# Product u in split parts, with VectorE's low parts at fixed places inside the convolution

## The chip, the cores and the metric

The kernel runs on one core of one Trainium2 chip. The metric is the time of one execution on the device in microseconds (us). The kernel before took 1014.25 us (median of three runs, 1013.29 to 1018.42).

## The reference, cut to what matters

One layer of a streaming encoder: 512 prompt tokens and 32 sample tokens (544 together), model width 1024, all in 32-bit floats.

```
h = modulate(rms_norm(x), shift, scale)
z = h @ w_in + b_in                    # 1024 -> 6 * 1024: a (2 parts), u, v, gates (2 parts)
a = glu(z[a]); a = silu(layer_norm(depthwise_causal_conv(a, width 31)))
u, v = gelu(z[u]), gelu(z[v]); v = layer_norm(v)
y_b = (u * (w_s mixes v over 128-frame chunks)) @ w_b
y_a = a @ w_a
merged = sigmoid(z[gate A]) * y_a + sigmoid(z[gate B]) * y_b
x = x + g1 * (merged @ w_o)
x = x + g2 * hierarchical MoE(modulate(rms_norm(x)))   # 32 experts
y = modulate(rms_norm(x))
```

## The kernel before, in words

The five engines' programs are written out by hand, each in its own order, and meet at semaphores. The features lie on partitions: a 1024x544 matrix is eight tiles of 128x544. TensorE makes the input projection in this order: eight units for a (each unit is two products, the value and the gate half of one tile), the product for v, four units for u (two tiles each), then sixteen gates, two to a unit. Between the gates stand the transposes of the convolution's history (`histories`), the channel statistics (`over_features`) and the mixing matrices (`mix`). After that come the two branch projections with the modulation products between them, the output projection, the routing and the experts.

Two forms of product are in use. `product` (L509 on) takes the 32-bit operands as they are: eight steps over the inner dimension, two halves of 272 columns each, and each such matmul is two records of L515 in the trace. `product_split` (L575 on, matmul at L580) works on parts: a high part (the operand rounded to the format `fp32r`) and a low part (the operand less its high part, in the same format). It runs three matmuls in place of each one: high weights with high input, high weights with low input, low weights with high input. The kernel before uses it for the gates alone.

Weights of the input projection go through two buffers (`W`, `WP`, the same memory), 1 MB a unit. SP loads unit n once `w_used` says that TensorE is done with unit n - 2 (`unit_load`). The high parts of a unit's weights (`wH2`) lie in the second half of its buffer, the low parts (`wL2`) replace the weights in place. For the gates ScalarE makes the high parts (`high_gate`, copy at L978, counted in `gw_high`) and GpSimd the low parts (`low_gate`, L1605, counted in `gw_split`). The parts of the input h are `gH` (ScalarE, L955, all eight tiles after the last unit of a, counted in `g_high`) and `gL` (VectorE, L1243, all eight tiles after the convolution's sums, counted in `g_split`). `gate(0)` waits for `g_split`.

VectorE runs the depthwise convolution in a hardware loop (`Fori`, L1211) of four turns, two channel tiles a turn: four multiplies for the GLU (L1217), two `tensor_scalar` for tap 0 (L1225), and 60 `scalar_tensor_tensor` for taps 1 to 30 (L1228), each over 574 columns; every address in the loop comes from registers. After it come the sums over tiles (`add_tiles`, L1234, counted in `conv_sum`), `gL`, the statistics of v (L1249, L1250, counted in `v_var`), then, once ScalarE has taken the square roots (L1004, L1005), the reciprocal (L1255) and the normalised v (L1259, L1264, L1265), of which GpSimd does a share (L1613, L1615). Then the channel means are subtracted (L1269) and the mixed v is added and multiplied into u (L1278, L1281, L1284). L643 is the first matmul of `mix` and waits for `v_norm`.

ScalarE drains each product: L948 and L949 for a, L973 for v, L985 for u, L997 for the gates. After `gate(0)` it stores a history (L961 and a DMA at L963), then waits for `v_var` and takes the square roots, then goes on with `gate(1)` and the second history. TensorE's `over_features` (L650) waits for that second history copy.

Of the kernel before, what the change touches and what calls it, by code (L numbers as in the profile page):

```python
# [29 lines left out]
ds = bass.ds  # L30
# [41 lines left out]
def build(nc, a, y_out, hist_p_out, hist_s_out, v_out):  # L72
    with ExitStack() as ctx:
# [153 lines left out]
        w_full = [sem("w_full0"), sem("w_full1")]  # L227
        x2_in = sem("x2_in")
        bias_split, conv_sum = sem("bias_split"), sem("conv_sum")
        glu_ready, gate_ps, gate_drained, y_ps = sem("glu_ready"), sem("gate_ps"), sem("gate_drained"), sem("y_ps")  # L230
# [277 lines left out]
        def _(pe):  # L508
# [110 lines left out]

            pe.wait_ge(v_gelu, 10)  # L620
            for n in range(4):
                b = n % 2
                full(pe, U_U + n)
                pe.wait_ge(act_drained, Q_U + n - 1)
                for m in range(2):
                    last = product(4 * b + 2 * m, WP[b][:, m], hT)
                last.then_inc(w_used, 1)
# [256 lines left out]
        def _(act):  # L884
# [59 lines left out]
            for n in range(KT):  # L944
                b = 4 * (n % 2)
                act.wait_ge(w_used, U_A + n + 1)
                for bank, c0, w, at in ((b, 0, H, HIST), (b + 1, 0, NPROMPT - H, HIST + H), (b + 1, NPROMPT - H, NSAMPLE, 2 * HIST + NPROMPT)):
                    act.activation(aF[:, n, at:at + w], PS[:, bank, c0:c0 + w], ACT.Identity, bias=VT[:, COL_BIN + n:COL_BIN + n + 1]).then_inc(glu_ready, 1)  # L948
                act.activation(two(cv[:, n, 0:T]), PS[:, b + 2:b + 4, 0:H], ACT.Sigmoid,  # L949
                               bias=VT[:, COL_BIN + KT + n:COL_BIN + KT + n + 1]).then_inc(act_drained, 1)  # L950
            act.wait_ge(h_even, KT)
            act.wait_ge(h_odd, KT)
            act.wait_ge(bias_split, 3)
            for j in range(KT):
                act.activation(gH[:, j, :], hT[:, j, :], ACT.Copy).then_inc(g_high, 1)  # L955

# [8 lines left out]
            for g, (what, bank) in enumerate(zip(V_ORDER, V_BANK)):  # L965
                if g in (4, 8):
                    act.wait_ge(w_used, U_V + 1 + g // 8)
                else:
                    act.wait_ge(v_ps, g + 1 if g < 4 else g)
                for hf in (0, 1) if g == 2 else (what[1],):  # L970
                    src = PS[NSAMPLE * hf:NSAMPLE * (hf + 1), bank + hf, :] if g == 2 else PS[:, bank, :]
                    t = 4 if g == 2 else what[0]
                    act.activation(v[0:WIDTH[t], t, hf * 512:(hf + 1) * 512], src, ACT.Gelu_apprx_tanh).then_inc(v_gelu, 1)  # L973

            def high_gate(q):
                full(act, U_G + q)
                for m in range(2):
                    act.activation(wH2[q % 2][:, m], WP[q % 2][:, m], ACT.Copy).then_inc(gw_high, 1)  # L978

            for n in range(4):  # L980
                b = n % 2
                act.wait_ge(w_used, U_U + n + 1)
                for m in range(2):
                    j = 2 * n + m
                    last = act.activation(two(uT[:, j, :]), PS[:, 4 * b + 2 * m:4 * b + 2 * m + 2, 0:H], ACT.Gelu_apprx_tanh,  # L985
                                          bias=VT[:, COL_BIN + 2 * KT + j:COL_BIN + 2 * KT + j + 1])
                last.then_inc(act_drained, 1)
                if n == 2:
                    high_gate(0)

# [8 lines left out]

            high_gate(1)  # L1000
            gate(0)
# [119 lines left out]
        def _(dve):  # L1121
# [88 lines left out]

            with dve.Fori(0, KT // 2) as half:  # L1211
                i = half * 2
                dve.wait_ge(act_drained, i + (Q_A + 2))
                dve.wait_ge(glu_ready, i * 3 + 6)
                for b in range(2):
                    for at, w, first in ((HIST, NPROMPT, 0), (2 * HIST + NPROMPT, NSAMPLE, NPROMPT)):
                        dve.tensor_tensor(tile_of(aF, i + b, at, w), tile_of(aF, i + b, at, w), tile_of(cv, i + b, first, w),  # L1217
                                          ALU.mult).then_inc(aF_written, 1)
                dve.wait_ge(aF_written, i * 2 + 8)
                for k in range(TAPS):  # L1220
                    for b in range(2):
                        total, src = tile_of(cv, i + b, 0, CONV), tile_of(aF, i + b, k, CONV)
                        tap = VT[:, ds(i + (k * KT + b), 1)]
                        if k == 0:
                            dve.tensor_scalar(total, src, tap, VT[:, ds(i + (COL_CB + b), 1)], ALU.mult, ALU.add).then_inc(conv_step, 1)  # L1225
                        else:
                            dve.wait_ge(conv_step, i * TAPS + (2 * (k - 1) + b + 1))
                            dve.scalar_tensor_tensor(out=total, in0=src, scalar=tap, in1=total, op0=ALU.mult, op1=ALU.add).then_inc(conv_step, 1)  # L1228


# [9 lines left out]
            add_tiles(cv)  # L1240
            dve.wait_ge(g_high, KT)
            for j in range(KT):
                dve.tensor_tensor(gL[:, j, :], hT[:, j, :], gH[:, j, :], ALU.subtract).then_inc(g_split, 1)  # L1243
            dve.wait_ge(bc_in, 64)
# [325 lines left out]
        def _(pool):  # L1570
# [31 lines left out]
            def low_gate(q):  # L1602
                for m in range(2):
                    pool.wait_ge(gw_high, 2 * q + m + 1)
                    pool.tensor_tensor(wL2[q % 2][:, m], WP[q % 2][:, m], wH2[q % 2][:, m], ALU.subtract).then_inc(gw_split, 1)  # L1605
# [118 lines left out]
```

## Time and profile before

| What | Value |
|---|---|
| Median of three runs | 1014.25 us |
| The profiled execution's own time | 1014.02 us |
| Its span | 1012.2 us |
| Mean granted TensorE clock | 0.944 of full speed |
| TensorE matmul busy | 886.8 us, 88% |
| TensorE weight load busy | 619.2 us, 61% |
| VectorE busy | 464.1 us, 46% |
| ScalarE busy | 169.2 us, 17% |
| GpSimd busy | 150.1 us, 15% |
| HBM read, written | 206.31 MB, 15.37 MB |

The span runs from the first to the last instruction of the profiled execution; the execution's own time is 1.8 us more. Busy time is the union of an engine's instructions. In the rows further down, a timeline row gives start, duration, engine, line, operation, written and read tiles, shape and count; consecutive instructions of one form are merged, and the bracket gives the idle time of the engine ahead of the row and what ended it. Two instructions of one engine can overlap by a little, since the next starts while the last one's results are still being written.

### The profile page before, as it was taken

To read this page: it belongs to the slowest core of one execution; us is meant where nothing else is said; L and a number is where in the kernel's file an instruction comes from. 1 tells how busy PE (TensorE), PEld (TensorE's weight loads), DVE (VectorE), ACT (ScalarE), POOL (GpSimd) and SP (SyncE) were. 2 spreads that over 40 slices of the span, in tenths; PEclk is the share of its full clock that TensorE was granted. 3 is DMA by queue.
4 is the path that set the end of the run, shared out by engine and by line. 5 is a ranking of instruction groups with operands and counts; after the bars stand their busy time and mean duration, and the time that the engine had idled before them with its cause. 6 is when DMAs were issued, how large, how long until landed. Compare 5 with 4: busy or idle time off the path is not lost. (4 is left out here: it accounts for less than half of the span.)

```text
span 1012.2 us, 11883 instructions
## 1 busy us (share of the span) xinstructions
PE 886.8 (88%) x4633; PEld 619.2 (61%) x4636; DVE 464.1 (46%) x694; ACT 169.2 (17%) x262; POOL 150.1 (15%) x180
## 2 busy tenths in 40 slices
PE   2899999999997979899999999817998898877846
PEld 1688885348887979776666544515666565544512
DVE  2329999999929361201112143571332233223127
ACT  3210113100142114500000011201121111101003
POOL 2000000000047083001111000002222222121110
PEclk9899999999998989999999999757999999989877
DMA  9912333003322133646758391434999999999943
GB/s 326 299 54 73 84 92 116 25 17 84 84 76 64 43 125 84 218 158 260 286 203 297 113 344 41 157 130 168 417 419 417 416 404 410 365 376 414 368 158 130
DMA packets 96116, 210.41 MB, mean 208 GB/s; under 512 B 10412, under 2 KB 52756, under 8 KB 87358
## 3 DMA queue, kind: packets, MB, share of 16 engines
q1 hardware_dynamic: 69776, 138.29, 37.5%
q10 hardware_dynamic: 13374, 37.03, 9.5%
q0 software_dynamic: 12912, 34.33, 9.3%
q8 instruction: 39, 0.64, 0.3%
q14 instruction: 15, 0.12, 0.0%
HBM read 206.31 MB, written 15.37 MB: 219 GB/s over the span
## 5 line engine op out<-in xcount | busy, mean ns | idle before, releaser
L515 PE MATMUL PS<-arena 128*128 128x272 f32 x1280 | 299.2, 395 | 4.2 <-issue 1.9
L515 PEld LDWEIGHTS PS<-arena 128*128 128x128 f32 x1280 | 243.1, 191 | 65.3 <-issue 14.1
L826 PE MATMUL PS<-arena 128*64 128x256 f32 (+1 forms) x1088 | 153.1, 404 | 26.1 <-issue 24.7
L1228 DVE SCALAR_TENSOR_TENSOR arena<-arena,VT x240 | 174.8, 807 | 0.0
L826 PEld LDWEIGHTS PS<-arena 128*64 128x64 f32 (+1 forms) x1088 | 114.3, 155 | 60.2 <-issue 34.8
L1605 POOL TENSOR_TENSOR wL<-arena,wH 128x1024 fp32r<-128x1024 f32 x16 | 38.2, 2408 | 282.6 <-ACT wH L978 282.5
L846 PE MATMUL PS<-arena 128*64 128x512 f32 (+1 forms) x272 | 72.7, 597 | 6.3 <-issue 4.6
L1502 DVE TENSOR_TENSOR arena<-PS,arena 128x256 f32<-128x256 f32 x20 | 8.5, 425 | 138.3 <-ACT arena L1067 138.3
L1679 POOL DMA_INDIRECT pairs<-arena,sidx x20 | 32.2, 1609 | 201.3 <-DVE arena L1518 201.3
L580 PE MATMUL PS<-gH,wH 128*128 128x272 f32 x256 | 55.1, 297 | 7.2 <-POOL wL L1605 5.6
L617 PE MATMUL PS<-arena 128*128 128x512 f32 x128 | 56.2, 592 | 2.2 <-ACT arena L949 1.9
L725 PE MATMUL PS<-arena 128*128 128x512 f32 x128 | 55.5, 593 | 1.3 <-DVE mrow L1318 1.3
L580 PE MATMUL PS<-gH,wL 128*128 128x272 f32 x256 | 53.9, 292 | 0.0
L580 PE MATMUL PS<-gL,wH 128*128 128x272 f32 x256 | 53.9, 292 | 0.0
L846 PEld LDWEIGHTS PS<-arena 128*64 128x64 f32 (+1 forms) x272 | 24.4, 146 | 40.0 <-issue 38.8
L580 PEld LDWEIGHTS PS<-gH,wH 128*128 128x128 f32 x256 | 41.0, 193 | 8.1 <-POOL wL L1605 5.8
L1067 ACT ACTIVATE arena<-PS 128x256 f32<-128x256 f32 x20 | 7.7, 384 | 219.6 <-PE PS L826 219.6
L725 PEld LDWEIGHTS PS<-arena 128*128 128x128 f32 x128 | 24.1, 190 | 31.4 <-issue 31.4
L617 PEld LDWEIGHTS PS<-arena 128*128 128x128 f32 x128 | 24.3, 190 | 29.0 <-issue 28.8
L580 PEld LDWEIGHTS PS<-gH,wL 128*128 128x128 f32 x256 | 41.0, 192 | 0.0
L580 PEld LDWEIGHTS PS<-gL,wH 128*128 128x128 f32 x256 | 40.9, 192 | 0.0
L1304 DVE TENSOR_TENSOR arena<-PS,arena 128x544 f32<-128x544 f32 x8 | 5.8, 725 | 66.3 <-PE PS L515 66.3
(271 smaller groups left out, 790.1 us busy)
## 6 DMA issues: line engine op xcount, KB each, us to landing
arena<-w_gate SPq DMA_DIRECT2D x34, 1024.0 KB, 12.4
arena<-w_up SPq DMA_DIRECT2D x34, 1024.0 KB, 18.8
arena<-w_down ACTq DMA_DIRECT2D x30, 1024.0 KB, 21.2
arena<-w_in SPq DMA_DIRECT2D x40, 512.0 KB, 5.2
arena<-w_ada SPq DMA_DIRECT2D x4, 2048.0 KB, 20.8
vecs<-w_ada POOLq DMA_DIRECT2D x4, 2048.0 KB, 9.7
arena<-w_ada POOLq DMA_DIRECT2D x4, 2048.0 KB, 8.7
arena<-x_prompt SPq DMA_DIRECT2D x8, 512.0 KB, 10.5
```

Of the source, the lines that this page charges most:

```text
L515: last = pe.matmul(PS[:, bank + h, 0:H], tile_w[:, k, :], act[:, k, h * H:(h + 1) * H], start=(k == 0), stop=(k == KT - 1))
L580: last = pe.matmul(PS[:, bank + h, 0:H], w[:, k, :], part[:, k, h * H:(h + 1) * H], start=(k == 0 and n == 0), stop=(k == KT - 1 and n == 2))
L617: last = pe.matmul(PS[:, bank, :], hT[:, k, t * P:(t + 1) * P], W[hf][:, k, :], start=False, stop=(k == KT - 1))
L725: last = pe.matmul(PS[:, (2 * t + hf) % 8, :], mT[:, k, t * P:(t + 1) * P], W[hf][:, k, :], start=(k == 0), stop=(k == KT - 1))
L826: last = pe.matmul(PS[h * rows:(h + 1) * rows, 2, n * DE:(n + 1) * DE], hG[:, b, k * SLOTS + h * rows:k * SLOTS + (h + 1) * rows], buf[r / ...
L846: last = pe.matmul(PS[h * rows:(h + 1) * rows, 4 + 2 * b + hf, :], heT[:, k, h * rows:(h + 1) * rows], WD[r // 2][r % 2][:, k, hf * 512:(h ...
L1067: act.activation(sil, PS[:, 2, 0:DE], ACT.Silu).then_inc(sil_ready, 1)
L1228: dve.scalar_tensor_tensor(out=total, in0=src, scalar=tap, in1=total, op0=ALU.mult, op1=ALU.add).then_inc(conv_step, 1)
L1304: dve.tensor_tensor(m_j, y, two(gB[:, j, :]), ALU.mult).then_inc(dve_drained, 1)
L1502: dve.tensor_tensor(he, PS[:, 2, DE:2 * DE], sil, ALU.mult).then_inc(he_ready, 1)
L1605: pool.tensor_tensor(wL2[q % 2][:, m], WP[q % 2][:, m], wH2[q % 2][:, m], ALU.subtract).then_inc(gw_split, 1)
L1679: pool.indirect_dma_start(out=pairs, out_offset=bass.IndirectOffsetOnAxis(ap=sidx[b][:, 0:1], axis=0), in_=Y[:, b, :], in_offset=None, bou ...
```

## The change

The product for u takes the split form. ScalarE makes the high parts of h in pairs between the units of a (after units 2 to 5), not all at once behind them, and the high parts of u's weights (`high_of`) after the seventh group of v, after the last group, and after each unit of u; the same function then serves the first gates. VectorE makes the low parts of h and of u's weights (`low_u`). Their places are fixed in its program: h's after the second pair of channel tiles, u's unit 0 after the third pair, and units 1, 2 and 3 after taps 9, 17 and 25 of the last pair. For that the convolution's loop is written out, with constant addresses. A new semaphore `u_split` counts u's low parts, and TensorE waits for it before each product of u; it no longer waits for u's transfers itself. The wait for `g_split` stands ahead of u. GpSimd's `low_gate` counts `gw_high` from eight on.

```
@@ -618,12 +619,13 @@
                 last.then_inc(w_used if g in (4, 8) else v_ps, 1)
 
             pe.wait_ge(v_gelu, 10)
+            pe.wait_ge(g_split, KT)
             for n in range(4):
                 b = n % 2
-                full(pe, U_U + n)
                 pe.wait_ge(act_drained, Q_U + n - 1)
                 for m in range(2):
-                    last = product(4 * b + 2 * m, WP[b][:, m], hT)
+                    pe.wait_ge(u_split, 2 * n + m + 1)
+                    last = product_split(4 * b + 2 * m, wH2[b][:, m], wL2[b][:, m], gH, gL)
                 last.then_inc(w_used, 1)
 
             def gate(j):
@@ -948,11 +950,17 @@
                     act.activation(aF[:, n, at:at + w], PS[:, bank, c0:c0 + w], ACT.Identity, bias=VT[:, COL_BIN + n:COL_BIN + n + 1]).then_inc(glu_ready, 1)
                 act.activation(two(cv[:, n, 0:T]), PS[:, b + 2:b + 4, 0:H], ACT.Sigmoid,
                                bias=VT[:, COL_BIN + KT + n:COL_BIN + KT + n + 1]).then_inc(act_drained, 1)
-            act.wait_ge(h_even, KT)
-            act.wait_ge(h_odd, KT)
-            act.wait_ge(bias_split, 3)
-            for j in range(KT):
-                act.activation(gH[:, j, :], hT[:, j, :], ACT.Copy).then_inc(g_high, 1)
+                if n == 2:
+                    act.wait_ge(h_even, KT)
+                    act.wait_ge(h_odd, KT)
+                    act.wait_ge(bias_split, 3)
+                if n in (2, 3, 4, 5):
+                    for j in (2 * n - 4, 2 * n - 3):
+                        act.activation(gH[:, j, :], hT[:, j, :], ACT.Copy).then_inc(g_high, 1)
+            def high_of(n):
+                full(act, n)
+                for m in range(2):
+                    act.activation(wH2[n % 2][:, m], WP[n % 2][:, m], ACT.Copy).then_inc(gw_high, 1)
 
             def store_history(n, dst):
                 act.wait_ge(hist_ps, n + 1)
@@ -971,11 +979,12 @@
                     src = PS[NSAMPLE * hf:NSAMPLE * (hf + 1), bank + hf, :] if g == 2 else PS[:, bank, :]
                     t = 4 if g == 2 else what[0]
                     act.activation(v[0:WIDTH[t], t, hf * 512:(hf + 1) * 512], src, ACT.Gelu_apprx_tanh).then_inc(v_gelu, 1)
+                if g == 6:
+                    high_of(U_U)
+            high_of(U_U + 1)
 
             def high_gate(q):
-                full(act, U_G + q)
-                for m in range(2):
-                    act.activation(wH2[q % 2][:, m], WP[q % 2][:, m], ACT.Copy).then_inc(gw_high, 1)
+                high_of(U_G + q)
 
             for n in range(4):
                 b = n % 2
@@ -985,8 +994,7 @@
                     last = act.activation(two(uT[:, j, :]), PS[:, 4 * b + 2 * m:4 * b + 2 * m + 2, 0:H], ACT.Gelu_apprx_tanh,
                                           bias=VT[:, COL_BIN + 2 * KT + j:COL_BIN + 2 * KT + j + 1])
                 last.then_inc(act_drained, 1)
-                if n == 2:
-                    high_gate(0)
+                high_of(U_U + n + 2)
 
             def gate(j):
                 c, dst = (COL_BIN + 5 * KT + j, gB) if j < KT else (COL_BIN + 4 * KT + j - KT, gA)
@@ -997,7 +1005,6 @@
                 act.activation(two(dst[:, j % KT, :]), PS[:, 2 * (j % 2):2 * (j % 2) + 2, 0:H], ACT.Sigmoid,
                                bias=VT[:, c:c + 1]).then_inc(gate_drained, 1)
 
-            high_gate(1)
             gate(0)
             store_history(0, hist_p_out)
             act.wait_ge(v_var, 1)
@@ -1208,25 +1215,36 @@
             def tile_of(buf, j, c0, n):
                 return buf[:, ds(j, 1), c0:c0 + n].rearrange("p o t -> p (o t)")
 
-            with dve.Fori(0, KT // 2) as half:
-                i = half * 2
+            def low_u(n):
+                for m in range(2):
+                    dve.wait_ge(gw_high, 2 * n + m + 1)
+                    dve.tensor_tensor(wL2[n % 2][:, m], WP[n % 2][:, m], wH2[n % 2][:, m], ALU.subtract).then_inc(u_split, 1)
+
+            for i in range(0, KT, 2):
                 dve.wait_ge(act_drained, i + (Q_A + 2))
                 dve.wait_ge(glu_ready, i * 3 + 6)
                 for b in range(2):
                     for at, w, first in ((HIST, NPROMPT, 0), (2 * HIST + NPROMPT, NSAMPLE, NPROMPT)):
-                        dve.tensor_tensor(tile_of(aF, i + b, at, w), tile_of(aF, i + b, at, w), tile_of(cv, i + b, first, w),
+                        dve.tensor_tensor(aF[:, i + b, at:at + w], aF[:, i + b, at:at + w], cv[:, i + b, first:first + w],
                                           ALU.mult).then_inc(aF_written, 1)
                 dve.wait_ge(aF_written, i * 2 + 8)
                 for k in range(TAPS):
                     for b in range(2):
-                        total, src = tile_of(cv, i + b, 0, CONV), tile_of(aF, i + b, k, CONV)
-                        tap = VT[:, ds(i + (k * KT + b), 1)]
+                        total, src, c = cv[:, i + b, :], aF[:, i + b, k:k + CONV], k * KT + i + b
+                        tap = VT[:, c:c + 1]
                         if k == 0:
-                            dve.tensor_scalar(total, src, tap, VT[:, ds(i + (COL_CB + b), 1)], ALU.mult, ALU.add).then_inc(conv_step, 1)
+                            dve.tensor_scalar(total, src, tap, VT[:, COL_CB + i + b:COL_CB + i + b + 1], ALU.mult, ALU.add).then_inc(conv_step, 1)
                         else:
                             dve.wait_ge(conv_step, i * TAPS + (2 * (k - 1) + b + 1))
                             dve.scalar_tensor_tensor(out=total, in0=src, scalar=tap, in1=total, op0=ALU.mult, op1=ALU.add).then_inc(conv_step, 1)
-
+                    if i == 6 and k in (9, 17, 25):
+                        low_u((k - 1) // 8)
+                if i == 2:
+                    dve.wait_ge(g_high, KT)
+                    for j in range(KT):
+                        dve.tensor_tensor(gL[:, j, :], hT[:, j, :], gH[:, j, :], ALU.subtract).then_inc(g_split, 1)
+                if i == 4:
+                    low_u(0)
 
             def add_tiles(src):
                 dve.wait_ge(dve_step, steps_done[0])
@@ -1238,9 +1256,6 @@
 
             dve.wait_ge(conv_step, TAPS * KT)
             add_tiles(cv)
-            dve.wait_ge(g_high, KT)
-            for j in range(KT):
-                dve.tensor_tensor(gL[:, j, :], hT[:, j, :], gH[:, j, :], ALU.subtract).then_inc(g_split, 1)
             dve.wait_ge(bc_in, 64)
             for t in range(TT):
                 w = WIDTH[t]
@@ -1601,7 +1616,7 @@
 
             def low_gate(q):
                 for m in range(2):
-                    pool.wait_ge(gw_high, 2 * q + m + 1)
+                    pool.wait_ge(gw_high, KT + 2 * q + m + 1)
                     pool.tensor_tensor(wL2[q % 2][:, m], WP[q % 2][:, m], wH2[q % 2][:, m], ALU.subtract).then_inc(gw_split, 1)
 
             low_gate(0)

```

## Rows read from the trace of the kernel before

**Rows 1.** The page, busy time, share of the span and instructions of each engine.

```profile
PE 886.8 (88%) x4633; PEld 619.2 (61%) x4636; DVE 464.1 (46%) x694; ACT 169.2 (17%) x262; POOL 150.1 (15%) x180
```

**Rows 2.** Waits of TensorE from 225 us on: total us, times, longest us.

```profile
PE PS L580 <- POOL wL L1605: 5.6, 1, 5.6
...
PE PS L643 <- DVE arena L1265: 3.5, 1, 3.5
...
PE PS L650 <- ACT tmp L961: 2.1, 1, 2.1
```

**Rows 3.** Busy windows: L515 during u, L580 during two gates (us, busy, clock, DMA).

```profile
228.09:286.66 58.57, 58.57 (x256) 48.55 (x256) 1.00 0.26 72
...
380.44:392.55 12.11, 12.11 (x98) 12.04 (x96) 1.00 0.32 88
```

**Rows 4.** Timeline of the convolution: VectorE, and ScalarE's sigmoid ahead of it.

```profile
74.49 0.73 ACT L949 ACTIVATE arena<-PS,VT 128x544 f32<-128x544 f32 x1
...
75.61 1.50 DVE L1217 TENSOR_TENSOR arena<-arena  x4 [19.63 <-ACT arena L949]
77.39 1.07 DVE L1225 TENSOR_SCALAR arena<-arena,VT  x2 [0.28 <-DVE arena L1217]
78.37 43.71 DVE L1228 SCALAR_TENSOR_TENSOR arena<-arena,VT  x60
...
214.74 1.49 DVE L1217 TENSOR_TENSOR arena<-arena  x4
```

**Rows 5.** Timeline of all engines, 225 to 300 us.

```profile
227.44 0.60 ACT L973 ACTIVATE arena<-PS 128x512 f32<-128x512 f32 x1 [6.49 <-PE PS L617]
...
262.02 4.72 DVE L1234 TENSOR_TENSOR rstdc<-rstdc,arena 128x574 f32<-128x574 f32 x6
266.65 5.17 DVE L1243 TENSOR_TENSOR gL<-arena,gH 128x544 fp32r<-128x544 f32 x8
271.73 1.41 DVE L1249 BATCH_NORM_STATS2 bn<-arena 128x6 f32<-128x512 f32 x2
272.39 1.32 ACT L985 ACTIVATE arena<-PS,VT 128x544 f32<-128x544 f32 x2 [13.35 <-PE PS L515]
...
278.06 2.00 ACT L978 ACTIVATE wH<-arena 128x1024 fp32r<-128x1024 f32 x2 [4.34 <-DMA arena<-w_in]
...
278.52 1.40 DVE L1249 BATCH_NORM_STATS2 bn<-arena 32x6 f32<-32x512 f32 x2
279.19 4.66 POOL L1605 TENSOR_TENSOR wL<-arena,wH 128x1024 fp32r<-128x1024 f32 x2 [254.11 <-ACT wH L978]
279.95 0.20 DVE L1250 BATCH_NORM_AGGREGATE mv<-bn 32x2 f32<-32x12 f32 x1
...
293.82 4.75 POOL L1605 TENSOR_TENSOR wL<-arena,wH 128x1024 fp32r<-128x1024 f32 x2 [9.96 <-ACT wH L978]
```

**Rows 6.** Timeline of ScalarE, VectorE and TensorE, 298 to 320 us.

```profile
298.05 1.28 ACT L1004 ACT_TABLE_LOAD   x1 [0.44 <-ACT tmp L961]
299.35 0.30 ACT L1004 ACTIVATE vsd<-mv,eps 128x4 f32<-128x4 f32 x1
299.55 0.28 ACT L1005 ACTIVATE vsd<-mv,eps 32x1 f32<-32x1 f32 x1
...
299.86 0.19 DVE L1255 RECIPROCAL vsd<-vsd 128x5 f32<-128x5 f32 x1 [19.71 <-ACT vsd L1005]
...
319.72 2.08 PE L643 MATMUL PS<-wsT,arena 128*128 128x128 f32 x8 [3.51 <-DVE arena L1265]
```

**Rows 7.** Timeline of VectorE, 315 to 332 us, then of GpSimd.

```profile
315.19 1.23 DVE L1265 TENSOR_TENSOR arena<-arena,vecs 128x1024 f32<-128x1024 f32 x1
...
319.58 5.38 DVE L1269 TENSOR_TENSOR arena<-arena,PS 128x574 f32<-128x574 f32 x8
...
325.76 4.91 DVE L1284 TENSOR_TENSOR arena<-arena,tmp 128x544 f32<-128x544 f32 x1
...
331.48 0.72 DVE L1284 TENSOR_TENSOR arena<-arena,tmp 128x544 f32<-128x544 f32 x1
...
320.77 9.31 POOL L1605 TENSOR_TENSOR wL<-arena,wH 128x1024 fp32r<-128x1024 f32 x4
```

More of the change, by code:

```diff
@@ L228, in build @@
         x2_in = sem("x2_in")
+        u_split = sem("u_split")
         bias_split, conv_sum = sem("bias_split"), sem("conv_sum")
```

## The prediction

> **What bounds the kernel now.** I read the page's busy times first: TensorE is busy 88% of the span, VectorE 46% [rows 1]. An average hides where the limit changes hands, so next the waits of TensorE from 225 us on [rows 2]. Between the product for u and the end of the gates TensorE waits three times on a chain from elsewhere: for ScalarE's copy of a history before the channel statistics (L650), for VectorE's last step of v (L643), and for GpSimd's low parts (L580). So u itself is bound by TensorE, but what follows hangs on two chains at once: TensorE's own, and VectorE's: convolution, sums, statistics of v, normalised v, mix. The stretch of u is one unbroken run: 58.57 us for 256 records of L515 [rows 3].
>
> **TensorE's part.** A unit of u is two products. A unit of the gates, the same shapes in three split passes, takes 12.11 us at the full granted clock [rows 3]; u's unit takes 58.57 / 4 = 14.64. Four units at 12.11 are 48.44, so 10.13 us go if nothing waits.
>
> **VectorE's part.** The low parts of h (eight instructions of 0.72 us that start 0.64 apart: 5.17 us, 5.09 as a shift [rows 5]) move from behind the sums into the convolution. The low parts of u's weights are new: eight subtractions of 1024 columns. One such takes 1.23 us when alone [rows 7]; started 0.08 before the one ahead ends, as L1243 does, that is 1.14, so 2.28 a unit and 9.12 in all. The convolution also loses its loop. In it the first tensor_scalar starts 0.28 us after the multiply it waits for, where L1234, written without a loop, starts 0.035 after its predecessor (0.792 apart, 0.757 long) [rows 4, 5]; and the first multiply starts 0.39 after ScalarE's sigmoid (75.22 to 75.61), where L1255 follows ScalarE by 0.03 [rows 4, 6]. I put this down to the loop's register instructions: four times 0.24 and 0.35, a gain of 1.3 us. The taps themselves start (43.71 - 0.81) / 59 = 0.727 apart [rows 4], each before the last has ended, so their issue is already hidden and I give them the same price (bounds: nothing to 0.02 us each way).
>
> Now the clock times. The last pair of channel tiles began at 214.74 [rows 4]; less 1.07 (three of the four loop gaps and the first) it is 213.67, then h's low parts to 218.76 and unit 0's to 221.04, its first half done at 219.98, before u starts at 228.09. Multiply and first tap pair (2.74 before, 2.50 now) lead to 223.54; 18 taps to 236.63. There unit 1's low parts: first half at 237.85. Sixteen taps on, unit 2's at 251.76; sixteen more, unit 3's at 265.67. The last ten taps would end at 274.08, against 261.19 before.
>
> TensorE: unit 0 from 228.09 to 240.20, unit 1 to 252.31, unit 2 to 264.42: both low parts were there. Unit 3 waits until 265.72, 1.30 us, and ends at 277.83, not 286.66: 8.83 us earlier.
>
> Are the high parts in time? From ScalarE's gelu of a unit to its copy of the next weights 5.67 us pass (272.39 to 278.06; the transfer is in them), and a copy takes 1.0 [rows 5]. Unit 1's are there near 234.2 (227.44 + 5.67 + 1.06), before 236.63; unit 2's near 247.2, unit 3's near 259.3, each 3 to 5 us before VectorE asks. Behind VectorE's new waits stand the taps, and nobody but this chain waits for those. The copies of h (L955) and the copies put between the gelus fall into ScalarE's waits of 5 us and more for TensorE: nothing, and a copy that were late would hold the gelu behind it by at most 2 us, with no reader before the next unit.
>
> **What is late next.** The gates' first weights now come earlier too. GpSimd's first low part started 7.0 us after the end of u's third unit (272.19, which is 228.09 plus three units, to 279.19), and ran 4.66 us beside statistics that it left alone: L1249 kept 0.7 us each [rows 5]. Now it starts at 264.42 + 7.0 = 271.4, in the last taps. What GpSimd does to VectorE is in the trace: a multiply of two SBUF tensors (L1284) took 4.91 us while GpSimd's L1605 ran, and 0.72 right after; L1269, with one operand in PSUM, kept 0.66 from one to the next beside it [rows 7]. VectorE's instruction ended 0.6 after GpSimd's last one, 320.77 + 9.31. A tap (L1228) has two SBUF tensors too, but no row shows it beside GpSimd. Bounds: nothing, if taps pass as L1269 does, and 4.66 plus the 0.5 or so that a hand-over costs, 5.2. I take 4.6, by the nearer row, L1284: seven taps are started by 271.4, the eighth ends near 277.1, the tenth at 278.6 or 278.7.
>
> The Trainium skill, GPSIMD Engine Reference, Key points, says that GpSimd contends for its SBUF interfaces with VectorE instructions that have two SBUF inputs. By that rule the taps are held, which is the 4.6 above; by L1269's row alone they would not be, and the rival below applies.
>
> Sums: seven, 5.5 us, to 284.2. Statistics: 271.73 to 280.15 before, 8.42 us, so now 292.65. ScalarE takes them in L1004. Before, it got there by its own path, table load at 298.05 and first square root at 299.35, 19 us after VectorE was done [rows 6]. That path moves with TensorE: 299.35 - 8.83 = 290.5. So VectorE is now the later one, by 2.2 us, and the square root starts at 292.7, 6.65 us earlier than before. From there everything is released as before: square root, normalised v, mix; the history copy stands behind the square root on ScalarE, so the channel statistics (L650) and two gates move by the same 6.65. The wait of 3.5 us ahead of the first mix [rows 2] stays about as long.
>
> **The rest of the span.** Gates, projections, routing and experts are released from within the kernel, so they move as a block. The sum is 58.57 to 49.74 for u (-8.83), +2.2 for VectorE's chain: -6.6 us. The profiled execution took 1014.02 us, the median shown is 1014.25: from the one 1007.4, on the scale of the other 1007.6. I say 1007.5.
>
> **The rivals.**
> One: GpSimd does not hold the taps, or for less than 2.4 us. For it: L1249 and L1269 run on beside it. Against: L1284. Then the statistics end at 288.1, before 290.5, and TensorE's 8.83 us count in full: 1005.3.
> Two: GpSimd's second pair of low parts catches the sums. It starts near 277.83 + 7.1 = 284.9 (293.82 before, where VectorE sat idle [rows 5]), and the last sum starts at 283.4. If VectorE is 1.6 us later against TensorE than I have it, one sum is held for 4.7 us more: -1.9, 1012.1. For it: the margin is small; against: any delay ahead of unit 3's low part moves both.
> Three, the other side: the convolution written out runs slower per instruction than the loop. It executes 264 VectorE instructions read once instead of a body repeated four times, and each fixed place ties TensorE to it. Below 0.028 us per tap (6.6 / 240) it only eats the gain; at 0.05 it is 12 us, and the kernel is slower by 5: 1019.6. Against it: taps overlap by 0.08 us now.
> Four: part of the gain is given back downstream by the clock, as more of TensorE's idle time stands in one piece ahead of L650 (2.1 us before, 4.3 after). Two gates stand between it and the wait for v, and that wait covers 3.5 us. I give it 1 to 2 us at most: 1009.3.
>
> **How the numbers follow.** Chances: forecast 0.56, rival one 0.13, two 0.12, four 0.10, three 0.06, and 0.03 for a gain lost otherwise. 0.5% of the time, 5.07 us, is about what a measurement of this kernel can tell from no change: the border is 1009.2. Forecast (nearly all of it) and rival one lie below, half of four too: faster 0.68. Same: two, the rest of the forecast and of four: 0.25. Slower 0.07. Range: 1004.8, a little under rival one, to 1012.5, a little over rival two.
>
> **What would show it.** In the changed profile: u's four units near 12.1 us each and one wait of about 1.3 us ahead of the fourth, none ahead of the second and third; L1225's idle time down from 0.28; one tap near 271 us that lasts 4 to 5 us; L1004 ending an idle time of ScalarE that VectorE's L1250 releases; the first mix near 313 instead of 319.7 [rows 6]. I am wrong if the taps keep 0.727 beside GpSimd (then the gain is nearer 9), if a sum is held as well, or if ScalarE's copies come later than VectorE's fixed places, which would show as idle time of VectorE inside the convolution.

## The result

The changed kernel took 1007.78 us (median of six runs, 1005.80 to 1010.86) against 1013.98 us for the kernel before in the same comparison. The ratio of the runs is 0.9916, with a 95% interval of 0.9886 to 0.9945. Two later comparisons gave 0.9920 (0.9897 to 0.9944) and 0.9910 (0.9895 to 0.9926). The forecast was 1007.5 us in a range of 1004.8 to 1012.5.

The profiled execution took 1005.8 us and its span is 1003.8, against 1014.02 and 1012.2. Its busy line answers to [rows 1]: TensorE loses 9.3 us, VectorE gains 13.3.

```profile
PE 877.5 (87%) x4764; PEld 620.5 (62%) x4764; DVE 477.4 (48%) x702; ACT 177.2 (18%) x270; POOL 152.5 (15%) x180
```

TensorE's waits between 285 and 320 us answer to [rows 2]. Ahead of the channel statistics (now L652) it waits 3.7 us where it waited 2.1; ahead of the first mix 2.0 where it waited 3.5.

```profile
PE PS L652 <- ACT tmp L969: 3.7, 1, 3.7
PE PS L645 <- DVE arena L1284: 2.7, 1, 2.7
PE PS L645 <- DVE arena L1280: 2.0, 1, 2.0
```

The 1.5 us that this last wait lost are in the next fence. It shows busy windows from the channel statistics to the end of the two gates behind them, the kernel before first. Each row gives the window, its length, then for TensorE, its weight loads, VectorE, ScalarE and GpSimd the busy time and the instructions, then the granted clock, the share of the DMA engines and GB/s. The same 100 matmul records take 13.32 us before and 14.80 after. The granted clock was 1.00 in the first window and 0.89 in the second: right behind the wait of 3.7 us, from 295.40 to 298.90, it was 0.51, the lower of its two levels.

```profile
302.89:316.21 13.32, 13.31 (x100) 12.88 (x100) 13.18 (x6) 2.73 (x3) 10.30 (x4) 1.00 0.19 52
```

```profile
295.71:310.51 14.80, 14.80 (x100) 14.01 (x100) 14.63 (x8) 2.72 (x3) 10.26 (x4) 0.89 0.06 14
```

The next fence is the busy windows of the split matmul (L581) and its weight loads, as in [rows 3]. Four units of u fill 49.9 us instead of 58.57, and 1.2 us of that is idle; two gates still take 12.11.

```profile
228.10:278.00 49.90, 48.72 (x384) 48.53 (x385) 1.00 0.32 86
373.81:385.92 12.11, 12.11 (x98) 12.05 (x96) 1.00 0.32 88
```

Then the timeline of VectorE at the start of the convolution, as [rows 4], and around its end, as [rows 5]. L1221 is a low part of u, L1239 a tap, L1252 a sum, L1264 the statistics.

```profile
75.30 1.50 DVE L1228 TENSOR_TENSOR arena<-arena 128x512 f32<-128x512 f32 x4 [19.05 <-ACT arena L951]
76.84 1.07 DVE L1236 TENSOR_SCALAR arena<-arena,VT 128x574 f32<-128x574 f32 x2
77.82 43.70 DVE L1239 SCALAR_TENSOR_TENSOR arena<-arena,VT 128x574 f32<-128x574 f32 x60
...
264.49 2.35 DVE L1221 TENSOR_TENSOR wL<-arena,wH 128x1024 fp32r<-128x1024 f32 x2
266.76 7.35 DVE L1239 SCALAR_TENSOR_TENSOR arena<-arena,VT 128x574 f32<-128x574 f32 x10
274.15 2.83 DVE L1252 TENSOR_TENSOR rstdc<-arena 128x574 f32<-128x574 f32 x1
277.01 6.78 DVE L1252 TENSOR_TENSOR rstdc<-rstdc,arena 128x574 f32<-128x574 f32 x6
283.71 1.41 DVE L1264 BATCH_NORM_STATS2 bn<-arena 128x6 f32<-128x512 f32 x2
```

And GpSimd's two first low parts for the gates, each by itself:

```profile
271.72 4.64 POOL L1620 TENSOR_TENSOR wL<-arena,wH 128x1024 fp32r<-128x1024 f32 x1 [246.56 <-ACT wH L963]
276.32 2.89 POOL L1620 TENSOR_TENSOR wL<-arena,wH 128x1024 fp32r<-128x1024 f32 x1
```

Read these two fences together. The ten taps from 266.76 take 7.35 us, so each keeps its 0.727 although GpSimd's instruction is under way from 271.72. It is GpSimd's that is late: 4.64 us where two took 4.66 [rows 5], and it ends 2.25 us after the last tap. Then the first sum takes 2.83 us and the second as long; six sums fill 6.78 us where they filled 4.72 [rows 5].

Last, ScalarE's square root, VectorE's reciprocal and the first mix, as [rows 6]. The square root has idle time that VectorE's L1265 ends, and comes at 292.17 instead of 299.35.

```profile
289.33 1.28 ACT L1011 ACT_TABLE_LOAD   x1 [0.44 <-ACT tmp L969]
292.17 0.30 ACT L1011 ACTIVATE vsd<-mv,eps 128x4 f32<-128x4 f32 x1 [1.55 <-DVE mv L1265]
...
292.68 0.19 DVE L1270 RECIPROCAL vsd<-vsd 128x5 f32<-128x5 f32 x1 [0.55 <-ACT vsd L1012]
...
312.50 2.08 PE L645 MATMUL PS<-wsT,arena 128*128 128x128 f32 x8 [1.99 <-DVE arena L1280]
```

Where the time came from, in the profiled pair: 8.6 us at the first gate (286.66 to 278.02), 7.2 at the first mix, 6.5 when the gates end, 7.0 when the last stage's matmuls begin (981.81 to 974.84), and 8.4 at the end of the span. The last 1.4 us belong to those sixteen matmuls, 8.77 us instead of 10.18 in the rows below, which come from the chain of work that ended last. The changed kernel's own repeats take 8.5 to 10.1 us there, so that is not the change's.

```profile
981.81 10.18 PE PS L879 x16
```

```profile
974.84 8.77 PE PS L881 x16
```

### The profile page after: what moved, and what is told of

The parts are those of the page before. It is cut to its first block and busy times, and to the rows that moved or that the text cites. A ratio compares the mean times of both kernels' runs of the same rounds, so it can differ in the third digit from the quotient of the medians.

```text
span 1003.8 us, 11622 instructions
## 1 busy us (share of the span) xinstructions
PE 877.5 (87%) x4764; PEld 620.5 (62%) x4764; DVE 477.4 (48%) x702; ACT 177.2 (18%) x270; POOL 152.5 (15%) x180
## 5 line engine op out<-in xcount | busy, mean ns | idle before, releaser
L516 PE MATMUL PS<-arena 128*128 128x272 f32 x1024 | 240.6, 396 | 3.4 <-issue 1.9
L516 PEld LDWEIGHTS PS<-arena 128*128 128x128 f32 x1024 | 194.7, 191 | 54.0 <-issue 14.0
L1239 DVE SCALAR_TENSOR_TENSOR arena<-arena,VT 128x574 f32<-128x574 f32 x240 | 175.1, 808 | 0.0
L581 PE MATMUL PS<-gH,wH 128*128 128x272 f32 x384 | 82.0, 296 | 9.1 <-POOL wL L1620 5.6
L1620 POOL TENSOR_TENSOR wL<-arena,wH 128x1024 fp32r<-128x1024 f32 x16 | 41.0, 2590 | 271.3 <-ACT wH L963 271.2
L581 PE MATMUL PS<-gL,wH 128*128 128x272 f32 x384 | 81.1, 293 | 0.0
L581 PE MATMUL PS<-gH,wL 128*128 128x272 f32 x384 | 80.7, 292 | 0.0
L581 PEld LDWEIGHTS PS<-gH,wH 128*128 128x128 f32 x384 | 61.3, 192 | 11.2 <-POOL wL L1620 5.8
L581 PEld LDWEIGHTS PS<-gH,wL 128*128 128x128 f32 x384 | 61.6, 192 | 0.0
L581 PEld LDWEIGHTS PS<-gL,wH 128*128 128x128 f32 x384 | 61.6, 193 | 0.0
L727 PEld LDWEIGHTS PS<-arena 128*128 128x128 f32 x128 | 24.1, 190 | 31.4 <-issue 31.4
L618 PEld LDWEIGHTS PS<-arena 128*128 128x128 f32 x128 | 24.3, 190 | 29.0 <-issue 28.8
## 6 DMA issues: line engine op xcount, KB each, us to landing
arena<-w_gate SPq DMA_DIRECT2D x34, 1024.0 KB, 13.3
```

What stands on the lines that cost most here:

```text
L516: last = pe.matmul(PS[:, bank + h, 0:H], tile_w[:, k, :], act[:, k, h * H:(h + 1) * H], start=(k == 0), stop=(k == KT - 1))
L581: last = pe.matmul(PS[:, bank + h, 0:H], w[:, k, :], part[:, k, h * H:(h + 1) * H], start=(k == 0 and n == 0), stop=(k == KT - 1 and n == 2))
L618: last = pe.matmul(PS[:, bank, :], hT[:, k, t * P:(t + 1) * P], W[hf][:, k, :], start=False, stop=(k == KT - 1))
L727: last = pe.matmul(PS[:, (2 * t + hf) % 8, :], mT[:, k, t * P:(t + 1) * P], W[hf][:, k, :], start=(k == 0), stop=(k == KT - 1))
```

## The experiments

The theory after the result: two chains lead to the square roots of v, TensorE's with ScalarE behind it and VectorE's; the change shortens the first by 8.7 us and lengthens the second until it is the later one by 1.55. The rivals: TensorE's chain alone sets the time; or VectorE's already did; and for the hold between GpSimd and VectorE, that the two take turns also during the taps. Executions differ in when the convolution begins: the first multiply stands at 74.1 to 76.5 us, and at 75.30 in the first trace of the changed kernel. So positions are compared after taking the offset to 75.30 away where it is named.

**The changed kernel as base (after_control, after_again).** No edit.

> The changed kernel itself, as the base for the other runs. Both theories: about 6.2 us faster than the kernel before (medians 1013.98 and 1007.78 so far). In its trace the square root of v's statistics starts near 292.2 us, released by VectorE, and u ends at 278.0 us.

> The changed kernel once more, on one chip with the candidate, to tell the two apart by time as well: about 7 us faster than the kernel before.

Measured: medians 1008.29 and 1006.58, against 1015.92 and 1015.88 for the kernel before. The second trace has its square root at 292.02; the first began 1.2 us late and has it at 293.39. Both sums are held in both (2.83 and 2.82, 2.83 and 2.83), so the hold is no chance of one execution. The slower stretch behind the wait ahead of L652 is in both too: 14.87 and 16.01 us for the same 100 records, at a granted clock of 0.89 and 0.82.

**Padding VectorE in both kernels (pad_before, pad_after).** The same seven instructions ahead of v's statistics:

```
+            dve.wait_ge(v_gelu, 10)
+            for _ in range(7):
+                then(dve.bn_stats(bn[:, 0, :], v[:, 0, 0:512]))
```

> The kernel before with seven extra bn_stats on VectorE (0.73 us each, 5.1 us in all, results overwritten) ahead of v's statistics. Theory: VectorE has 19 us of slack there, so statistics end near 285.3 and the time is unchanged (within 0.5 us in the trace). Rival (VectorE's chain already counted): up to 5.1 us slower.

> The changed kernel with the same seven extra bn_stats (5.1 us). Theory: VectorE's chain now sets the square roots, so all of it counts: they start near 297.3 and the kernel is 5.1 us slower than the changed one, about 1 us faster than the one before. Rival (TensorE's path sets it, or slack is left): under 2 us slower.

Measured on ScalarE's timeline, the kernel before with padding first, then the changed one with it:

```profile
298.00 1.28 ACT L1004 ACT_TABLE_LOAD   x1 [0.44 <-ACT tmp L961]
299.29 0.30 ACT L1004 ACTIVATE vsd<-mv,eps 128x4 f32<-128x4 f32 x1
```

```profile
289.43 1.28 ACT L1011 ACT_TABLE_LOAD   x1 [0.44 <-ACT tmp L969]
297.24 0.30 ACT L1011 ACTIVATE vsd<-mv,eps 128x4 f32<-128x4 f32 x1 [6.53 <-DVE mv L1268]
```

Before, 5.1 us more on VectorE move nothing (299.35 to 299.29); the ratio is 1.0005 (0.9982 to 1.0028). After, they move the square root by 5.07 us, and the ratio is 0.9983 (0.9956 to 1.0010) where the changed kernel has 0.991 to 0.992. The changed kernel itself was not run in this comparison, so the 5.1 us are read from the trace; the times only agree with them. This shows that VectorE's 19 us of slack are used up, and both halves came out as the theory had them.

**The low parts of u two and four taps earlier (places_earlier).**

```
-                    if i == 6 and k in (9, 17, 25):
-                        low_u((k - 1) // 8)
+                    if i == 6 and k in (9, 16, 23):
+                        low_u((k - 2) // 7)
```

> The changed kernel with VectorE's low parts of units 2 and 3 after taps 16 and 23 in place of 17 and 25; the work is the same. Unit 3's first low part is ready at 262.8 us, ahead of unit 2's end, so TensorE's wait of 1.1 us inside u goes and u ends near 276.8. Theory (VectorE's chain sets the end): the square root still starts near 292.2 and the time equals the changed kernel's within 0.3 us inside the trace. Rival (TensorE sets it): 1.2 us faster.

TensorE's wait inside u is gone and the first gate starts at 275.48; with the offset of this execution (its first multiply at 74.13, not 75.30) that is 276.65, 1.4 us earlier. The square root is at 291.00, and 292.17 with the offset: not moved. TensorE's wait ahead of L652 took it all, 5.1 us for 3.7:

```profile
PE PS L652 <- ACT tmp L969: 5.1, 1, 5.1
```

The ratio, 0.9925 (0.9899 to 0.9952), is that of the changed kernel. So the stall of 1.1 us inside u cost nothing, and up to the square root TensorE's chain is not the one that counts.

**Statistics ahead of the sums (stats_first).** The call of `add_tiles(cv)`, with its wait, moves behind the loop over v's statistics.

> The changed kernel with v's statistics (10 bn_stats, 5 bn_aggr) ahead of the convolution's sums on VectorE; the work is the same. Theory: statistics run beside GpSimd unheld and end near 282.5 us, so ScalarE's own path releases the square root at 290.6 (1.5 us earlier). But the sums now run from 282.6 and meet GpSimd's second pair of low parts at 285.1: two sums are held about 2.1 us each, they end near 292.2, and VectorE takes up the square roots hardly earlier than in the changed kernel (292.7): 0 to 0.5 us faster in all. Rival (GpSimd's hold of two sums is chance or not a hold): sums end at 288.1 and the gain is 1.5 us.

The statistics run unheld beside GpSimd's first pair and end at 282.87, and the square root starts at 291.22 with no idle time of ScalarE ahead of it, as expected (290.6; the offset is 0.4). VectorE's timeline of the sums, then GpSimd's:

```profile
282.80 0.71 DVE L1252 TENSOR_TENSOR rstdc<-arena 128x574 f32<-128x574 f32 x1
283.54 8.87 DVE L1252 TENSOR_TENSOR rstdc<-rstdc,arena 128x574 f32<-128x574 f32 x6
292.33 0.18 DVE L1270 RECIPROCAL vsd<-vsd 128x5 f32<-128x5 f32 x1
```

```profile
285.69 5.32 POOL L1620 TENSOR_TENSOR wL<-arena,wH 128x1024 fp32r<-128x1024 f32 x2 [6.55 <-ACT wH L963]
```

Now GpSimd's second pair holds two sums, by 2.1 us each (2.83 and 2.84 for 0.76). The reciprocal is 0.75 us earlier than in the changed kernel, its offset of 0.4 included; I had expected 0 to 0.5. The time is the same (0.9922, 0.9894 to 0.9951). The hold moves with the order, and its size was foretold.

**GpSimd waits for the sums (gpsimd_waits).**

```
+            pool.wait_ge(conv_sum, 1)
             low_gate(0)
```

> The changed kernel with GpSimd waiting for the convolution's sums before it makes the gates' first low parts. This takes away the hold of two sums (4.1 us of VectorE) and puts the same time on TensorE's side. Theory (two chains, the later one sets the square roots): sums end near 279.6 us with all seven at 0.76, the first gate starts near 282.1 in place of 278.0, statistics end near 288.1, and the square root now starts on ScalarE's own path near 294.6, 2.4 us later than in the changed kernel. Rival (only VectorE's chain counts): the square root starts near 288.1, 4.1 us earlier.

One execution was timed (1009.77 us), so this rests on its trace. All seven sums take 0.76, the first gate starts at 281.99 after TensorE has waited 4.1 us for GpSimd, and the square root comes at 293.45 with no idle time of ScalarE ahead of it: TensorE's chain is the later one again. I expected 294.6, and the 1.1 us between are, to 0.3 us, what is left of two larger things that I had left out. Behind the wait the granted clock was 0.53 for 3.56 us, and the first gate took 7.6 us (281.99 to 289.63) where it took 6.1 in the changed kernel. Against that, ScalarE had its copies and its table load behind it when this gate ended, where in the changed kernel it came to the gate 3.2 us after its end; it made up 3.0 us (its L1005 waits 2.86 us for TensorE). At the square root this cure is 1.3 us worse than the hold (293.45 to 292.17), in one execution.

```profile
PE PS L581 <- POOL wL L1620: 4.1, 1, 4.1
...
PE PS L652 <- ACT tmp L969: 1.2, 1, 1.2
```

```profile
281.99:285.55 3.56, 3.56 (x17) 3.56 (x18) 3.35 (x7) 1.89 (x2) 2.94 (x2) 0.53 0.28 65
```

**The convolution written out alone (unroll_only).** The kernel before with the changed kernel's taps and constant addresses, and nothing else of the change.

> The kernel before with the convolution written out and nothing else changed. Theory: each tap still starts 0.727 us after the last; the four gaps of 0.28 us ahead of the first tensor_scalar and the 0.39 us ahead of the first multiply shrink to about 0.03 to 0.08, the convolution ends 1.2 to 1.3 us earlier (near 259.9), and the time stays as it was, since VectorE waits 19.7 us for the square roots anyway. Rival (the loop's instructions held the taps back): taps closer than 0.72 us, or a change of the whole time.

VectorE's timeline at the start of the convolution:

```profile
76.05 1.07 DVE L1224 TENSOR_SCALAR arena<-arena,VT 128x574 f32<-128x574 f32 x2
77.03 43.71 DVE L1227 SCALAR_TENSOR_TENSOR arena<-arena,VT 128x574 f32<-128x574 f32 x60
120.66 1.49 DVE L1216 TENSOR_TENSOR arena<-arena 128x512 f32<-128x512 f32 x4
```

A pair of tiles takes 46.15 us from first multiply to first multiply (74.51 to 120.66) instead of 46.39 [rows 4]: 0.24 less, as worked out, and the taps are the same 43.71 for 60. The convolution ends at 259.15 for 261.19; 0.7 us of that is this execution's earlier start (its first gate, untouched by the edit, is at 285.92 for 286.66), and 1.3 is the edit's. The square root, at 298.66, is earlier by the 0.7 alone. The ratio is 0.9982, with an interval (0.9963 to 1.0002) that takes in no change. Rival three of the prediction falls with this.

**GpSimd makes u's low parts (u_low_on_gpsimd).** `low_u` is taken out of VectorE's program and the same eight subtractions stand at the head of GpSimd's.

> The changed kernel with all eight low parts of u's weights made by GpSimd in order, none by VectorE; the low parts of h stay. Two theories of the port. Stream (as one gap of the changed kernel's trace suggests: GpSimd's first instruction took 4.64 us and ended when the taps did, while the taps kept 0.727): back-to-back taps keep GpSimd out, it gets in only where VectorE pauses, at the edge of a pair of tiles. Then it takes one low part at the last edge (near 220 us), the second only when the taps end near 265, and TensorE waits some 30 us inside u: about 20 to 25 us slower than before. Alternation (as held instructions take turns elsewhere): each of the eight holds a tap for 2.3 to 2.9 us, the taps end near 283 instead of 274, TensorE waits little: 5 to 10 us slower than the changed kernel.

GpSimd's first four low parts in the timeline, then TensorE's longest wait, then VectorE's taps in the same stretch:

```profile
214.78 6.79 POOL L1621 TENSOR_TENSOR wL<-arena,wH 128x1024 fp32r<-128x1024 f32 x1 [189.71 <-ACT wH L963]
221.53 2.92 POOL L1621 TENSOR_TENSOR wL<-arena,wH 128x1024 fp32r<-128x1024 f32 x1
235.51 35.92 POOL L1621 TENSOR_TENSOR wL<-arena,wH 128x1024 fp32r<-128x1024 f32 x1 [11.06 <-ACT wH L963]
271.40 2.89 POOL L1621 TENSOR_TENSOR wL<-arena,wH 128x1024 fp32r<-128x1024 f32 x1
```

```profile
PE PS L581 <- POOL wL L1621: 31.3, 1, 31.3
```

```profile
233.52 35.72 DVE L1239 SCALAR_TENSOR_TENSOR arena<-arena,VT 128x574 f32<-128x574 f32 x49
```

One subtraction of GpSimd took 35.92 us: from its start to the end of the taps at 269.24, and then its own 2.2. The taps beside it kept 0.727. TensorE waited 31.3 us, and the kernel took 1040.94 us, ratio 1.0238 (1.0193 to 1.0284). Alternation falls for the taps, and the stream theory holds in what it says of them: beside them GpSimd cannot make u's low parts in time, VectorE can.

In its reason the stream theory is not shown. It has GpSimd wait for a pause of VectorE. Two low parts, not the expected one, got in at the edge of the last pair of tiles, and there VectorE did not pause. These are two of its multiplies for the GLU:

```profile
218.64 0.68 DVE L1228 TENSOR_TENSOR arena<-arena 128x512 f32<-128x512 f32 x1
219.24 2.38 DVE L1228 TENSOR_TENSOR arena<-arena 128x32 f32<-128x32 f32 x1
```

The first begins 0.08 us before the last tap ends and the second 0.08 before the first ends, just as the taps follow each other; yet GpSimd came in, and the second, of 32 columns, took 2.38 us. The changed kernel's normalised v shows the same: the third `tensor_scalar` there begins 0.07 us before the second ends and is held, 2.85 us instead of 0.81.

```profile
293.87 2.79 POOL L1628 TENSOR_TENSOR arena<-arena,vecs 128x1024 f32<-128x1024 f32 x1 [4.01 <-DVE arena L1274]
...
294.36 2.85 DVE L1274 TENSOR_SCALAR arena<-arena,mv,vsd 128x1024 f32<-128x1024 f32 x1
```

So it is this stream of taps that keeps GpSimd out, and not every stream without a pause. Which property of a tap does it (its operation, its operands, its length), no run here varies.

**A balanced version (balanced, balanced_again).** Statistics ahead of the sums, places after taps 9, 16 and 23, and the second gate unit's low parts on VectorE behind the sums, no longer on GpSimd. TensorE's waits are adapted. The new lines on VectorE:

```
+            for m in range(2):
+                dve.wait_ge(gw_high, KT + 2 + m + 1)
+                dve.tensor_tensor(wL2[1][:, m], WP[1][:, m], wH2[1][:, m], ALU.subtract).then_inc(u_split, 1)
```

> Candidate version: the changed kernel with statistics ahead of the sums, unit 2's and 3's places after taps 16 and 23, and the low parts of the second gate unit's weights made by VectorE behind the sums (two subtractions of 1024 columns) and not by GpSimd. Theory: no two-input instruction of VectorE meets GpSimd between 274 and 290 us; sums end at 288.1, the low parts at 290.4, the square root starts at 289.4, VectorE takes it up at 290.4 in place of 292.7: 2.3 us faster than the changed kernel. Rival (TensorE or something further on sets the time): no faster than the changed kernel.

> The candidate once more: the trace gave VectorE's reciprocal 2.3 us earlier than in the changed kernel, so about 9 us faster than the kernel before and 2.3 us faster than the changed one by medians. Rival: no difference beyond the spread of the medians (about 1 us).

VectorE's timeline in the first of the two traces:

```profile
282.45 0.71 DVE L1255 TENSOR_TENSOR rstdc<-arena 128x574 f32<-128x574 f32 x1
283.20 4.71 DVE L1255 TENSOR_TENSOR rstdc<-rstdc,arena 128x574 f32<-128x574 f32 x6
287.83 2.35 DVE L1274 TENSOR_TENSOR wL<-arena,wH 128x1024 fp32r<-128x1024 f32 x2
290.42 0.19 DVE L1276 RECIPROCAL vsd<-vsd 128x5 f32<-128x5 f32 x1 [0.24 <-ACT vsd L1015]
```

No sum is held, and the reciprocal is at 290.42, 2.3 us earlier, as expected. In the second trace it is 1.9 us earlier (289.62, with its offset of 1.2), and there ScalarE is the later one by 0.69 us. By time a gain over the changed kernel is not shown: medians 1005.22 and 1007.10 against the changed kernel's 1008.29 and 1006.58, ratios 0.9909 (0.9882 to 0.9936) and 0.9902 (0.9886 to 0.9918). The two traces show how much can go astray behind the gates. At the end of the gates they are 7.8 and 8.9 us ahead of the kernel before; at the last stage's first matmul the first is still 8.7 us ahead, the second only 2.1. The busy windows from 720 to 960 us, first trace and second, show the same granted clock, 0.94, and from 400 to 440 us it is 0.96 in both; only from 640 to 720 us is it lower in the second, 0.69 for 0.72. So the clock in these windows does not account for the 6.8 us, and their cause stays open.

```profile
720.00:960.00 240.00, 211.53 (x1290) 135.00 (x1288) 64.95 (x84) 33.66 (x50) 48.66 (x63) 0.94 0.97 389
```

```profile
720.00:960.00 240.00, 209.26 (x1296) 136.59 (x1294) 63.81 (x83) 32.28 (x48) 49.12 (x64) 0.94 0.98 394
```

## Why the prediction was right, step by step

- **TensorE's part: right.** u was forecast to end at 277.83 with one wait of 1.30 us ahead of the fourth unit; it ended at 278.02 with one of 1.1.
- **VectorE's part: right.** Unit 3's first low part was forecast for 265.67 and came at 265.70; the last tap for 274.08 if unheld, and it ended at 274.11. The loop's price was confirmed alone.
- **High parts in time: right, by less than I had.** No idle time of VectorE stands inside the convolution. But I gave each unit 3 to 5 us, and my own times leave unit 1 only 2.4 (234.2 to 236.63). Its first high part was there at 235.50, 1.2 us before VectorE took it at 236.68.
- **GpSimd's hold: near in size, wrong in place, and the sum right by luck.** I had the taps held for 4.6 us. No tap was: the stream of taps kept GpSimd out for 2.4 us, and then the first two sums were held, 2.83 + 2.83 - 2 x 0.76 = 4.1 us. The taps and the sums stand in one chain, so for the time it does not matter which of them waits. That both come to nearly the same was not foreseen: the prediction names as signs of being wrong that the taps keep 0.727, and that a sum is held as well, and both came. Rival one had the taps right; its 1005.3 us failed because it left the sums unheld. Where statistics stand behind the taps in place of the sums (stats_first), GpSimd's first pair holds nothing. The row I went by, L1284, was of an instruction that began while GpSimd already ran. It could not show what happens when GpSimd arrives in the middle of a stream.
- **What is late next: right.** Square root forecast at 292.7, measured 292.17; released by VectorE, as the padding shows.
- **The rest as a block: right to about 1 us up to the last stage in this pair, not in every execution.** The balanced kernel's second trace loses 6.8 us on the way that its first does not.
- **Rival four: its loss came, and was covered.** Behind the wait ahead of L652 (3.7 us; I had 4.3) the granted clock was 0.51 for 3.5 us, and TensorE took 1.5 us more to the end of the next two gates. The wait for v behind them, which I said would stay about 3.5 us long, shrank to 2.0 and covered it. In after_again the same stretch took 16.01 us and 0.8 us of that wait was left, so not much more could have been covered.
- **The waits: misread, with no effect on the sum.** I counted three waits of TensorE on other engines between u and the end of the gates. The profile has five: it also waits 2.7 us for VectorE's L1269 and 1.6 us for ScalarE's L997.
- **Rival two** did not occur: the sums ended at 283.79, ahead of GpSimd's second pair at 285.10. In stats_first it does.

The forecast of 6.6 us compares with 6.2, 7.6 and 9.3 us between medians and 7.2 in the trace at the square root. The medians of one kernel differ by up to 2 us between comparisons, so no finer test of the sum is to be had from them. The trace is finer: 8.73 us gained on TensorE's chain less 1.55 us of waiting for VectorE, where I had 8.83 less 2.2.

## What to carry to other kernels

When a change shortens one engine's stage and pays with another engine's slack, work out both chains to the place where they meet, and add up the idle time there: 19 us of slack went to less than nothing here, and 1.55 us of the gain with it. Work that is to be done beside a long stream of taps like these belongs into that stream at fixed places, not on GpSimd. When a wait of TensorE gets longer, price the stretch behind it at the lower clock level too: 1.5 us here, and 1.6 in gpsimd_waits. Stalls ahead of the meeting point that the later chain covers, such as the 1.1 us inside u, are not worth mending alone.

## What the hardware showed that I had not expected

- A GpSimd subtraction of 1024 columns that starts during the taps (start to start 0.727 us, each begun 0.08 before the last one ended) does not end until they are over: 35.92 us in one case, 6.79 and 4.64 in others, instead of 2.35. A pause of 0.035 us let it in behind them, but at the start of the next pair of tiles it came in with no pause (the multiply at 219.24).
- The sums, chained with a wait and 0.035 us apart, take turns with GpSimd's subtractions: 0.76 us become 2.83. This does not hold everywhere. The multiply L1299 below, L1284 of the kernel before, stayed held while GpSimd went from one subtraction straight to the next, and took 4.91 us. What decides between the two is not shown.

```profile
318.21 2.34 POOL L1620 TENSOR_TENSOR wL<-arena,wH 128x1024 fp32r<-128x1024 f32 x1
318.55 4.91 DVE L1299 TENSOR_TENSOR arena<-arena,tmp 128x544 f32<-128x544 f32 x1
320.51 2.35 POOL L1620 TENSOR_TENSOR wL<-arena,wH 128x1024 fp32r<-128x1024 f32 x1
```

- The Trainium skill, GPSIMD Engine Reference, Key points, names the contention of GpSimd with VectorE instructions that have two SBUF inputs. The sums bear it out. Beside the taps, which have two as well, it fell on GpSimd alone: VectorE kept its 0.727 us.
- Statistics (L1264) pass beside GpSimd at 0.68 to 0.70 us each, as they do alone.
- After waits of 3.7 and 4.1 us TensorE's granted clock was at its lower level for 3.5 us (0.51 behind L652 in the changed kernel, 0.53 in gpsimd_waits). After the 2.1 us ahead of L650 in the kernel before it stayed at 1.00. The length of the wait alone does not tell: it fell behind 2.3 us in stats_first (0.51 from 295.60 to 299.10), and not behind 2.7 us in the first trace of balanced (1.00 from 293.50 to 308.00).
